# A search over 60 pair sums instead of 256, more dot products inside it, and 128 chunks in other groups

## The reference

```python
def peer(h, w_query, sub_keys1, sub_keys2, expert_u, expert_v):
    q = (hf @ w_query).reshape(T, PEER_HEADS, 2, PEER_QDIM // 2)
    s1 = jnp.einsum('thc,hkc->thk', q[:, :, 0], sub_keys1)
    s2 = jnp.einsum('thc,hkc->thk', q[:, :, 1], sub_keys2)
    v1, i1 = lax.top_k(s1, PEER_TOPK)
    v2, i2 = lax.top_k(s2, PEER_TOPK)
    cand = (v1[..., :, None] + v2[..., None, :]).reshape(T, PEER_HEADS, 256)
    vc, ic = lax.top_k(cand, PEER_TOPK)
    e1 = jnp.take_along_axis(i1, ic // PEER_TOPK, axis=-1)
    e2 = jnp.take_along_axis(i2, ic % PEER_TOPK, axis=-1)
    idx = e1 * N_KEYS + e2
    gate = jax.nn.softmax(vc, axis=-1)
    # then, for each token, with u = expert_u[idx]:
    a = gelu(x . u) * gate
    out = sum over the 128 picks of a * expert_v[idx]
```

## Time and profile before

| | |
|---|---|
| median of 3 runs | 3519.72 us (3516.33 to 3525.31) |
| profiled execution | 3530.3 us |
| its span, first to last instruction | 3528.5 us |
| mean granted TensorE clock | 0.967 of full |
| TensorE, VectorE, ScalarE, GpSimd busy | 3273.5, 2324.7, 1333.6, 1372.3 us |
| first split of the stage, last gelu | 447.5, 1162.4 us |

### The profile page before, as it was taken

One profiled execution on the slowest core, in us unless ns is written; L12 is line 12 of the kernel. 1 busy time (PEld: TensorE's weight loads), 2 busy tenths in 40 slices (PEclk: granted clock), 3 DMA queues, 4 the chain that ended last, 5 costly groups with the idle time before them and its releaser, 6 DMA issues. The chain is left out here.

```text
span 3528.5 us, 51497 instructions
## 1 busy us (share of the span) xinstructions
PE 3273.5 (93%) x18667; PEld 2835.8 (80%) x18667; DVE 2324.7 (66%) x4662; ACT 1333.6 (38%) x2000; POOL 1372.3 (39%) x738
## 2 busy tenths in 40 slices
PE   7878999997998999999899889899989988899998
PEld 5756799987998999999686567688878866668877
DVE  7753978999997788888685566754551067644440
ACT  3434233334554433333312675322231145743331
POOL 3114446665765422222130564222223322444433
PEclk9988999999999999999999999999999999999999
DMA  6412546666999999999365503212211132033322
GB/s 214 145 39 85 178 138 221 216 208 215 360 371 380 340 370 365 364 359 340 103 195 135 88 5 114 90 60 65 59 51 58 53 108 73 28 130 94 94 77 89
DMA packets 235687, 588.97 MB, mean 167 GB/s; under 512 B 52548, under 2 KB 113988, under 8 KB 231405
## 3 DMA queue, kind: packets, MB, share of 16 engines
q1 hardware_dynamic: 177964, 419.63, 36.2%
q0 software_dynamic: 36864, 134.23, 10.4%
q10 hardware_dynamic: 20672, 32.68, 2.5%
HBM read 529.03 MB, written 56.91 MB: 166 GB/s over the span
## 5 line engine op out<-in xcount | busy, mean ns | idle before, releaser
L433 POOL TENSOR_TENSOR ahead_low<-w_raw,ahead_high 128x1024 fp32r<-128x1024 f32 (+1 forms) x159 | 426.6, 2683 | 891.9 <-ACT ahead_high L369 891.9
L229 PE MATMUL psum<-h_high,ahead_high 128*128 128x512 f32 (+1 forms) x1384 | 493.6, 357 | 3.4 <-POOL ahead_low L433 3.4
L230 PE MATMUL psum<-h_low,ahead_high 128*128 128x512 f32 (+1 forms) x1384 | 490.8, 355 | 0.0
L231 PE MATMUL psum<-h_high,ahead_low 128*128 128x512 f32 (+1 forms) x1384 | 489.4, 354 | 0.0
L369 ACT ACTIVATE ahead_high<-w_raw 128x1024 fp32r<-128x1024 f32 (+1 forms) x159 | 178.0, 1120 | 751.4 <-PE psum L231 719.5
L2070 POOL TENSOR_TENSOR pick_u_low<-pick_u_raw,pick_u_high 128x1024 fp32r<-128x1024 f32 x128 | 310.4, 2426 | 217.6 <-ACT pick_u_high L2189 217.0
L229 PE MATMUL psum<-peer_h_high,pick_u_high 128*128 128x384 f32 x1024 | 355.0, 347 | 24.1 <-POOL pick_u_low L2070 23.6
L230 PE MATMUL psum<-peer_h_low,pick_u_high 128*128 128x384 f32 x1024 | 348.7, 341 | 0.0
L231 PE MATMUL psum<-peer_h_high,pick_u_low 128*128 128x384 f32 x1024 | 346.1, 338 | 0.0
L229 PEld LDWEIGHTS psum<-h_high,ahead_high 128*128 128x128 f32 x1384 | 260.2, 188 | 44.3 <-issue 5.1
L231 PEld LDWEIGHTS psum<-h_high,ahead_low 128*128 128x128 f32 x1384 | 261.3, 189 | 40.5
(11 more groups left out here) (431 smaller groups left out, 8195.5 us busy)
## 6 DMA issues: line engine op xcount, KB each, us to landing
pick_u_raw<-in_expert_uT SPq DMA_DIRECT2D x128, 512.0 KB
v_raw<-in_expert_v SPq DMA_DIRECT2D x128, 512.0 KB
mod_w<-in_w_mod SPq DMA_DIRECT2D x88, 512.0 KB, 4.1
w_raw<-in_ffn_up SPq DMA_DIRECT2D x84, 512.0 KB, 3.6
gelu_dram<-pick_gelu ACTq DMA_DIRECT2D x128, 192.0 KB
gates_dram<-gate_plane SPq DMA_DIRECT2D x24, 1024.0 KB
g<-gates_dram SPq DMA_DIRECT2D x31, 768.0 KB
w_raw<-in_ffn_down SPq DMA_DIRECT2D x29, 704.0 KB, 4.0
```

What stands on the lines that cost most here:

```text
L229: nc.tensor.matmul(bank, w_high, x_high, start=first, stop=False)
L230: nc.tensor.matmul(bank, w_high, x_low, start=False, stop=False)
L231: return nc.tensor.matmul(bank, w_low, x_high, start=False, stop=last)
L433: nc.gpsimd.tensor_tensor(w_low[r % 2][:, :, :], raw[r % n_raw][:, :, :], w_high[r % 2][:, :, :].bitcast(F32), ALU.subtract).then_inc(k.w_ ...
```

## The change

It does five things. The pair sums are cut from 256 to the 60 that the table `PAIR_ROWS` covers, built for all 8 heads in four operations; their places are decoded with shifts, masks and comparisons. Of the dots, 16 are in each of the tiles 1 to 3 (after every second half and after each head), 48 in all. The exponential of tile i stands after chunk `EXP_CHUNKS[i]`: 12, 14, 15 and 17. The chunks are grouped 4 x 19, 44 and 8. The dots that remain, 80, are spread over 48 chunks, up to four before the last. The diff is whole.

```diff
--- before.py
+++ after.py
@@ -1737,24 +1737,27 @@
 DENSE = SEQ - P
 PLANES = DENSE // GATE_TOK
 FIND_TILES = (ROW_TILE, 0, 1, 2)
-FIND_CHUNKS, GATE_CHUNKS, LAST_CHUNKS = 18, 48, 8
+FIND_CHUNKS, GATE_CHUNKS, LAST_CHUNKS = 19, 44, 8
 GATES_AT = len(FIND_TILES) * FIND_CHUNKS
 LAST_AT = GATES_AT + GATE_CHUNKS
 GROUP_TOK = 4
 GROUPS = DENSE // GROUP_TOK
 PLANE_GROUPS = GATE_TOK // GROUP_TOK
 LEAD, STORE_PARTS = 3, 4
-SCORE_CHUNK, TURN_CHUNK, EXP_CHUNK = 11, 2, 16
+SCORE_CHUNK, TURN_CHUNK, EXP_CHUNKS = 11, 2, (12, 14, 15, 17)
 SPREAD_BANKS = 3
 U_RING, V_RING = 6, 4
-SEARCH_DOTS, HEAD_DOTS = {2: 2, 6: 4, 10: 6, 14: 9}, {1: 11, 3: 12, 5: 14, 7: 15}
-FIND_DOTS = (len(FIND_TILES) - 1) * (len(SEARCH_DOTS) + len(HEAD_DOTS))
-DOT_CHUNKS = GATE_CHUNKS + LAST_CHUNKS - 2
+TILE_DOTS = 2 * PEER_HEADS
+FIND_DOTS = (len(FIND_TILES) - 1) * TILE_DOTS
+DOT_CHUNKS = GATE_CHUNKS + LAST_CHUNKS // 2
 NEAR_CHUNK = 2 * TURN_CHUNK + 2
 PICK_KEYS_AT, PICK_U_AT = BIG + 2 * N_KEYS * GATE_TOK, 44760
 NA_QK_SPLIT = 42496
 ROWS_AT = NA_QK_SPLIT - 4 * PICKS
 VALUE_PAIR = 4
+PAIR_ROWS = ((0, 1, 16, 0), (1, 2, 8, 16), (3, 5, 4, 32), (8, 8, 1, 52))
+PAIRS = 60
+assert all(any(first <= i < first + n and j < width for first, n, width, _ in PAIR_ROWS) for i in range(TOPK) for j in range(TOPK) if (i + 1) * (j + 1) <= TOPK)
 MOD_COLS = 8
 assert LAST_AT + LAST_CHUNKS == N_KEYS
 
@@ -1772,7 +1775,7 @@
 
 def dot_chunks():
 
-    found = [FIND_CHUNKS * i + c for i in range(1, len(FIND_TILES)) for c in (*SEARCH_DOTS.values(), *HEAD_DOTS.values())]
+    found = [FIND_CHUNKS * i + (n + 1) * FIND_CHUNKS // TILE_DOTS - 1 for i in range(1, len(FIND_TILES)) for n in range(TILE_DOTS)]
     return found + [GATES_AT + q for q in range(DOT_CHUNKS) for _ in gate_dots(q)]
 
 
@@ -1955,11 +1958,11 @@
     rest = take("rest", N_KEYS)
     best_at = take("best_at", H2, TOPK, dtype=U32)
     best = take("best", H2, TOPK)
-    cand = take("cand", TOPK, TOPK)
-    cand_rest = take("cand_rest", TOPK * TOPK)
+    cand = take("cand", PEER_HEADS, PAIRS)
+    cand_rest = take("cand_rest", 64)[:, 0:PAIRS]
     top = take("top", PEER_HEADS, TOPK)
     top_at = take("top_at", PEER_HEADS, TOPK, dtype=U32)
-    half_at = [take(f"half_at{i}", PICKS, dtype=U32) for i in range(2)]
+    bits = [take(f"bits{i}", PICKS, dtype=U32) for i in range(5)]
     half_f = [take(f"half_f{i}", PICKS) for i in range(2)]
     equal = take("equal", PICKS // 2, TOPK)
     total = take("total", PEER_HEADS)
@@ -2215,7 +2218,7 @@
                         d = turn_parts[r]
                         act.wait_ge(rows_turned, r + 1)
                         nc.scalar.activation(h_rows[:, d[0] * P:(d[-1] + 1) * P], k.psum[:, 4, 0:len(d) * P], ACT.Copy).then_inc(h_rows_ready, 1)
-                    if r == EXP_CHUNK:
+                    if r == EXP_CHUNKS[i]:
                         act.wait_ge(shifted, i + 1)
                         nc.scalar.activation(out[2][:, :], out[2][:, :], ACT.Exp).then_inc(exped, 1)
             for q in range(GATE_CHUNKS):
@@ -2281,16 +2284,18 @@
                     best16(scores[:, n, :], rest[:, :], best[:, n, :], best_at[:, n, :])
                     if i > 1 and n == H2 // 2:
                         store_picks(i - 1)
-                    if i and n in SEARCH_DOTS:
+                    if i and n % 2:
                         dot()
                 dve.sem_inc(best_found, 1)
                 V(dve, nc.vector.tensor_copy(near, best[:, :, :].rearrange("p (h i) a -> p h i a", i=2)[:, :, 1, :]))
+                firsts = best[:, :, :].rearrange("p (h i) a -> p h i a", i=2)[:, :, 0, :]
+                for first, n, width, at in PAIR_ROWS:
+                    shape = [P, PEER_HEADS, n, width]
+                    V(dve, nc.vector.tensor_tensor(cand[:, :, at:at + n * width].rearrange("p h (n w) -> p h n w", w=width),
+                                                   firsts[:, :, first:first + n].unsqueeze(3).to_broadcast(shape), near[:, :, 0:width].unsqueeze(2).to_broadcast(shape), ALU.add))
                 for h in range(PEER_HEADS):
-                    first = best[:, 2 * h, :].unsqueeze(2).to_broadcast([P, TOPK, TOPK])
-                    second = near[:, h, :].unsqueeze(1).to_broadcast([P, TOPK, TOPK])
-                    V(dve, nc.vector.tensor_tensor(cand[:, :, :], first, second, ALU.add))
-                    best16(cand[:, :, :].rearrange("p a b -> p (a b)"), cand_rest[:, :], top[:, h, :], top_at[:, h, :])
-                    if i and h in HEAD_DOTS:
+                    best16(cand[:, h, :], cand_rest, top[:, h, :], top_at[:, h, :])
+                    if i:
                         dot()
 
                 weight = out[2][:, :].rearrange("p (h s) -> p h s", s=TOPK)
@@ -2299,12 +2304,18 @@
                 nc.vector.tensor_tensor(weight, top[:, :, :], top[:, :, 0:1].to_broadcast([P, PEER_HEADS, TOPK]), ALU.subtract).then_inc(shifted, 1)
 
                 where = top_at[:, :, :].rearrange("p h s -> p (h s)")
-                V(dve, nc.vector.tensor_scalar(half_at[0][:, :], where, 4, None, ALU.logical_shift_right))
-                V(dve, nc.vector.tensor_scalar(half_at[1][:, :], where, TOPK - 1, None, ALU.bitwise_and))
+                for x, op, n in zip(bits, (ALU.logical_shift_right, ALU.logical_shift_right, ALU.bitwise_and, ALU.bitwise_and, ALU.bitwise_and), (3, 2, 3, 4, 8)):
+                    V(dve, nc.vector.tensor_scalar(x[:, :], where, n, None, op))
+                V(dve, nc.vector.tensor_scalar(half_f[0][:, :], bits[0][:, :], 1.0, 0.0, ALU.subtract, ALU.max))
+                V(dve, nc.vector.scalar_tensor_tensor(half_f[0][:, :], bits[1][:, :], 5.0, half_f[0][:, :], ALU.subtract, ALU.max))
+                V(dve, nc.vector.scalar_tensor_tensor(half_f[0][:, :], where, 44.0, half_f[0][:, :], ALU.subtract, ALU.max))
+                V(dve, nc.vector.scalar_tensor_tensor(half_f[1][:, :], where, 52.0, bits[2][:, :], ALU.is_lt, ALU.mult))
+                for below, x in ((32.0, bits[3]), (16.0, bits[4])):
+                    V(dve, nc.vector.scalar_tensor_tensor(x[:, :], where, below, x[:, :], ALU.is_lt, ALU.mult))
+                    V(dve, nc.vector.tensor_tensor(half_f[1][:, :], half_f[1][:, :], x[:, :], ALU.add))
                 by_half = best_at[:, :, :].rearrange("p (h i) a -> p h i a", i=2)
                 for j in range(2):
                     V(dve, nc.vector.tensor_copy(number[j], by_half[:, :, j, :]))
-                    V(dve, nc.vector.tensor_copy(half_f[j][:, :], half_at[j][:, :]))
                 heads = PEER_HEADS // 2
                 for j in range(2):
                     for part in range(2):
```

## The result

The changed kernel takes **3551.29 us** (median of 4 runs, 3548.70 to 3558.40); the kernel before, on the same chip, 3521.43 (4 runs, 3516.33 to 3525.31). The ratio is 1.0085, 95% interval 1.0069 to 1.0101: slower by 30 us, where the forecast had 8.6 and a range that ended at 3541. The profiled execution took 3550.09 us (span 3548.3, clock 0.967), so it stands at its median, while that of before stood some 9 us above; the two profiled spans differ by 19.8 us. Lines up to the end of `best16` moved by three, those of the one-hots by eleven: the dot is L1840, the gathers L1832, the split L2073, the one-hots L2348 and L2352, the gates L2110.

What follows compares the result with a forecast made beforehand. VectorE's chain was taken to bound first search to last gate, DMA the tail, TensorE the value stage. First gate +39.7, gate stretch -23.8, tail -7.3 sum to +8.6 us on the median 3519.72: 3528 us, range 3498 to 3541.

Steps and rivals of the forecast that it cites:

- no loss: Search halves: dots 5.0 us apart, longer than a gather with its split (1.15 + 2.40), lose nothing.
- Candidates: VectorE's expert search: 60 pair sums for 256 save 10.3 us a tile.
- Decoding: After a tile's heads: 13 operations for 4 add 2.9 us; two splits cutting into them add 4.8 us.
- Tile 0: First search tile: ends 18 us earlier, about 517, but gain lost; gathers wait for chunk 20, first dot at 546.7.
- A dot against a split: Between heads: dots fall into step with GpSimd's splits, 4.33 us each, 1.47 lost; eight heads take 34.6 or 33.1 us.
- Sum to the first gate: VectorE's chain through tiles 1 to 3: first gate at 845.7 against 806 us, +39.7 us.
- the four cost nothing: Before the gates: four more TensorE chunks (17 us) are free, since VectorE comes 40 us later.
- Gate stretch: 19 dots fewer give -23.8 us; a chunk stays VectorE's by little, 6.2 us against TensorE's 6.1.
- Tail: Last eight chunks, bound by DMA: four row gathers instead of nine, 2.6 MB at 360 GB/s, -7.3 us.
- the third rival: Tail goes at TensorE's pace: -19 in place of -7.3 us, total -3, 3517 us; chance 0.15.
- dots slip between the splits: Rival, between heads: the loss of some 34 us shrinks to a third or nothing; about -17 to -22, 3500; chance 0.25.
- The full step: Rival, between heads: dot, gather and split in turn, 4.7 us a dot for 4.33; +20, 3540 us; chance 0.18.

Runs made afterwards that it cites:

- the cut alone: The kernel before with only the 60 pair sums and their decoding, its 8 dots a tile and 18/48/8 chunks kept: 3500.59 us, ratio to before 0.9932.
- the early rows: The changed kernel with the first six row gathers placed behind the split of chunk 15, not 20: 3537.41 us, ratio to before 1.0041.
- sixteen dots in the halves: The changed kernel with its 16 dots a tile put one after each half, none between the heads: 3565.40 us, ratio to before 1.0111.
- the PSUM run: The changed kernel with its 48 search dots reading their second operand from PSUM, giving wrong dot products: 3509.11 us, ratio to before 0.9955.
- with 8 dots: The changed kernel with 8 dots a search tile, four among the halves and four among the heads: 3513.97 us, ratio to before 0.9973.
- groups of 18: The changed kernel with chunks grouped 4 x 18, 48 and 8, not 4 x 19, 44 and 8: 3538.70 us, ratio to before 1.0055.

## Why the prediction was wrong in its size

The direction that it leaned to, and its mechanism, held; the size did not, and the time fell outside the range, above it. The steps that failed are "no loss" for the dots in the halves, in 5, where 11 us were lost, "it is still VectorE's by little" in 7, which made the gate stretch 7.7 us too short, and the size of the tail in 8. By its own steps:

1. *Candidates.* Tile 0, which has no dots, searched its eight heads in 11.9 us, 1.49 a head, and formed the sums in 1.25; reckoned were 1.53 a head and 1.3. Right. In the cut alone it is worth more than reckoned, for then the four dots between heads lose nothing.
2. and the second half of 5. *Decoding.* The rest of a tile took 24.6, 24.8 and 25.0 us against 25.4. Two operations of it were cut into by splits, in tile 1 by 2.1 and 2.2 us (the rows at 624.13 and 627.52). Right.
4. *Tile 0.* It ended at 517.46 (about 517), and the first dot began at 547.54 (546.7) after 23.54 us (25). Right; the early rows show that the gathers held it. In part this is luck: the stage began 1.9 us earlier than in the profile of before, and counted from there the first dot came 2.7 us later than reckoned.
5. *A dot against a split.* The mechanism is right: PSUM as the operand's place takes the loss away whole, and sixteen dots in the halves bring it there. The Trainium skill's rule in SBUF — State Buffer, section "SBUF: two separate sides", a lock between VectorE's operations with two SBUF inputs and GpSimd's in which the second fully blocks, agrees with this: 2.82 us with both inputs in SBUF, 1.22 with one in PSUM. The step was reckoned at 4.33 us a dot, and 4.35 is where each tile ends up, but only in the last two of its seven distances; the others run from 2.8 to 4.8 us, in tile 2 for instance 3.07, 4.72, 2.76, 4.07, 4.17, 4.35 and 4.35. The distance without a loss is 2.75 us, as the PSUM run shows, and not 2.86. So the heads came out shorter than forecast: with the copy and the sums they took 31.7, 33.4 and 35.6 us, where 33.1, 33.1 and 34.6 with 1.6 for those make 34.7, 34.7 and 36.2. The dots between heads lost 1.24 us each on the average, not 1.47.
6. *Sum to the first gate.* 851.7 for 845.7, **5.9 us short**, 7.9 counted from the first split. The step that failed is "no loss" in the halves. The eight dots there took 16.7, 11.9 and 12.2 us in tiles 1 to 3, where 9.8 is without loss: 11.3 us. The second dot of tile 1 met a gather and the split behind it (4.06 us), the third a split (3.08), and the eighth of every tile a split that had begun 0.05 to 0.2 us before it (3.42, 3.29 and 3.43).

   The premise was that 5.0 us between dots is longer than gather and split together. In these rows the two engines keep apart while GpSimd waits for a dot before it gathers, as it does behind the fourth dot of tile 2, for 1.6 us; before the split at 686.03 it had waited for ScalarE and not for a dot. That this is the cause was not tested. The halves were 6.8, 2.2 and 2.5 us over the forecast, heads and sums 3.0, 1.3 and 0.6 under, the rests 0.8, 0.6 and 0.4 under, and the first dot 0.8 late: that the sum missed by only 5.9 owes something to luck.

   That "the four cost nothing" holds where VectorE is late by as much as 19.5 us at the first gate; with 8 dots it is not late, and they do cost. With groups of 18 the first one-hot came 8 to 12 us earlier. Of this 2.5 to 5.3 us are the first dot's, and the eight dots in the halves of tiles 2 and 3 took 9.8 and 9.9 us, without a loss: the grouping also moves the splits and gathers against the dots. Why 18 gives the better phase was not tried further.
7. *Gate stretch.* Forecast -23.8, measured 286.4 - 302.5 = -16.1: **7.7 us short**. VectorE's own work fell as reckoned, from 299.4 to 275.2 us, 24.2 less. What failed is "it is still VectorE's by little": a mean over chunks hid that with 44 chunks eight carry three groups. VectorE waits 8.7 us for TensorE in seven places, and TensorE 31.5 - 19.5 = 12 us for VectorE in thirteen others. The groups of 18 show it, where this turns into TensorE's pace alone.
8. *Tail.* Forecast -7.3, measured 49.0 - 53.7 = **-4.7**: DMA is busy as said (0.95), but it moved 352 GB/s and not 360. TensorE's pace, the third rival, would have been 34 us. What took the missing 2.6 us no run shows.

The three misses are 5.9 + 7.7 + 2.6 = 16.2 us, and 8.6 + 16.2 = 24.8: the last gelu stood at 1187.0 for 1162.4, 24.6 later. The value stage handed this on (its end came 23.3 us later); at the end of the profiled span 19.8 were left, and the medians differ by 30. For these differences no step is to blame that a run shows. They are of the size by which executions differ with the same code, as behind the last gelu, and before's profile stood 9 us above its median. Adding a difference to the median carries that scatter, and the range should have had it.

Of the rivals, *dots slip between the splits* is what the cut alone does, with a dot after every second head, and what the changed kernel does not. *The full step* appears in places, between heads once in tiles 1 and 2 (4.74 and 4.72 us) and three times in tile 3, and in the halves of the run with sixteen there. Each case priced one thing going wrong; that the halves, the gate stretch and the tail could all come out late together, as they did, had no case, and so the range ended at 3541.

## What to carry to other kernels

When VectorE's operations with two SBUF inputs run beside GpSimd's, look at the distance from one to the next against the period of the other engine, not at the mean loss. At 4.25 us against 4.24 a dot was nearly always free. At 2.75 each dot put in cost 3.3 us of the first gate's time, and at 3.1 a dot took 2.4 us. At 5.0 most were free and some were not: a longer distance than the period is no safety by itself. Shortening the work between dots (here heads of 60) can make the loss per dot larger, and eight more dots a tile cost 34 to 37 us, although the 30 us of their own time come off the gate stretch again. The piece of the change that removed work gained 22 us; the rest, which moved work, cost some 50, and an uneven split of groups (96 on 44) cannot be judged by its mean.

## What the runs showed of the hardware

- An operation that waits for a gather and the split behind it waits for both: the dot of 552.52 lost 2.83 us, more than a split lasts. The first dot of the run with eight dots took 6.39 us, with two splits in a row beside it (4.66 us from 551.14). GpSimd's gather does not always stretch: 0.96 us when the dot was already waiting or done, 1.76 when the dot ran first.
- Operations of 128 values are held as long as dots: 2.38 us for 0.29 in the decoding. With the second operand in PSUM neither side is held, not even by a gather or a split that covers the whole of the dot: 48 dots at 1.221 us.
- Two engines that block each other settle into a steady step, here 4.35 us, but how they get there varies: heads of tile 2 took 33.4 and 36.3 us in two executions of the same kernel.
